# Rotary partners: copies on ScalarE in place of a rotation product on TensorE

## The reference

```python
def apply_rope(x, cos, sin):
    ...
    x1, x2 = x[..., :ROPE_AXIS], x[..., ROPE_AXIS:]      # 32 and 32 of a head's 64
    return jnp.concatenate([x1 * c - x2 * s, x1 * s + x2 * c], axis=-1)

q = apply_rope(rms_norm(q, q_gain), cos, sin) * (HEAD_DIM ** -0.5)
k = apply_rope(rms_norm(k, k_gain), cos, sin)
```

## Time and profile before

| | us |
|---|---|
| median of 3 runs | 1077.39 |
| profiled execution | 1076.99 |
| its span, first to last instruction | 1075.10 |
| TensorE busy | 1055.5 (98%) |
| VectorE busy | 686.2 (64%) |
| ScalarE busy | 547.3 (51%) |
| GpSimd busy | 90.5 (8%) |

### The profile page before, as it was taken

The page is one execution under the profiler, slowest core; times in us unless marked ns, Lnnn a source line. Parts: engine busy times, 40 slices in busy tenths (PEclk is TensorE's granted clock), DMA queues, the critical chain, the costliest instruction groups (busy, mean ns, idle before and its releaser), DMA issues.

```text
span 1075.1 us, 20694 instructions
## 1 busy us (share of the span) xinstructions
PE 1055.5 (98%) x8454; PEld 1025.9 (95%) x8454; DVE 686.2 (64%) x998; ACT 547.3 (51%) x790; POOL 90.5 (8%) x88
## 2 busy tenths in 40 slices
PE   9999999999999999999999999999999999999997
PEld 8999999999779999999999999999999999999986
DVE  6666656467674866664467666644698668667652
ACT  5444444454765544434346444444568846454541
POOL 2100000028000200000011000000224210000000
PEclk9999999999999999999999999999999999999999
DMA  9564446625013255445663564366328525655541
GB/s 299 164 223 159 137 145 204 220 96 171 21 41 127 96 191 176 156 127 188 195 196 118 179 195 155 108 213 208 118 80 268 163 79 181 201 168 195 192 141 39
DMA packets 160910, 170.15 MB, mean 158 GB/s; under 512 B 3264, under 2 KB 154104, under 8 KB 160840
## 3 DMA queue, kind: packets, MB, share of 16 engines
q1 hardware_dynamic: 160456, 168.70, 48.4%
q0 software_dynamic: 96, 0.28, 0.1%
q10 hardware_dynamic: 288, 0.18, 0.1%
HBM read 167.82 MB, written 1.05 MB: 157 GB/s over the span
## 4 chain that ended last, share of the span: by engine, by line
PE 89%; DVE 5%; ACT 3%; DMA 1%; POOL 1%; issue 1%; SPq 0%; DVEq 0%; POOLq 0%; ACTq 0%
PE bank L457 23%; PE bank L459 23%; PE bank L458 23%; PE bank L863 5%; PE bank L665 2%; PE bank L664 2%; PE bank L666 2%; PE bank L476 1%; PE bank L473 1%; PE bank L474 1%; PE weighed L768 1%; DMA raw<-in_rec_w_in 1%; DVE h L1414 1%; PE flipped L756 1%; POOL hacc L1865 1%; DVE xl L1378 1%
## 5 line engine op out<-in xcount | busy, mean ns | idle before, releaser
L1372 DVE TENSOR_TENSOR wl<-raw,wh 128x2048 fp32r<-128x2048 f32 (+2 forms) x164 | 342.2, 2108 | 152.5 <-ACT wh L962 152.2
L457 PE MATMUL bank<-xh,wl 128*128 128x272 f32 (+1 forms) x1488 | 430.6, 289 | 3.4 <-DVE tmp L1442 1.1
L459 PE MATMUL bank<-xh,wh 128*128 128x272 f32 (+1 forms) x1488 | 427.4, 287 | 0.0
L458 PE MATMUL bank<-xl,wh 128*128 128x272 f32 (+1 forms) x1488 | 425.8, 286 | 0.0
L962 ACT ACTIVATE wh<-raw 128x2048 fp32r<-128x2048 f32 (+2 forms) x164 | 282.2, 1745 | 105.3 <-PE bank L459 82.9
L457 PEld LDWEIGHTS bank<-xh,wl 128*128 128x128 f32 x1488 | 280.3, 188 | 5.2 <-issue 2.7
L458 PEld LDWEIGHTS bank<-xl,wh 128*128 128x128 f32 x1488 | 280.3, 188 | 0.0
L459 PEld LDWEIGHTS bank<-xh,wh 128*128 128x128 f32 x1488 | 280.3, 188 | 0.0
L457 PE MATMUL bank<-ah,wl 128*128 128x272 f32 x528 | 152.1, 288 | 0.0
L458 PE MATMUL bank<-al,wh 128*128 128x272 f32 x528 | 151.9, 288 | 0.0
L459 PE MATMUL bank<-ah,wh 128*128 128x272 f32 x528 | 151.7, 287 | 0.0
(11 more groups left out here) (197 smaller groups left out, 1209.9 us busy)
## 6 DMA issues: line engine op xcount, KB each, us to landing
raw<-in_ffn_w_in SPq DMA_DIRECT2D x88, 1024.0 KB, 5.3
raw<-in_ffn_w_out SPq DMA_DIRECT2D x24, 768.0 KB, 4.9
raw<-in_ffn_w_out SPq DMA_DIRECT2D x24, 640.0 KB, 4.4
raw<-in_ffn_w_out SPq DMA_DIRECT2D x10, 1024.0 KB, 5.2
raw<-in_rec_w_in SPq DMA_DIRECT2D x8, 1024.0 KB, 5.5
raw<-in_attn_w_qkv SPq DMA_DIRECT2D x6, 1024.0 KB, 5.0
raw<-in_attn_w_o SPq DMA_DIRECT2D x4, 1024.0 KB, 5.3
raw<-in_rec_gate_w SPq DMA_DIRECT2D x16, 256.0 KB, 5.2
```

The source lines that it names most:

```text
L457: pe.matmul(dst, b, mh, start=first, stop=False)
L458: pe.matmul(dst, a, ml, start=False, stop=False)
L459: return pe.matmul(dst, a, mh, start=False, stop=last)
L1372: dve.tensor_tensor(wl[:, slot(u), 0:kn * 256], w, wh[:, slot(u), 0:kn * 256].bitcast(F32), ALU.subtract).then_inc(w_ready, units)
```

## The change

The rotation product goes. In its place ScalarE copies the partner rows of `qp` into `pad`, in four blocks of 32 partitions and 272 columns for each tile: rows 32 to 63 into 0 to 31, 0 to 31 into 32 to 63, and the same in the upper half. The minus sign moves into the sine table. VectorE's `times_sin` then multiplies `pad` in place, reading it from SBUF instead of the product from PSUM. The wait for `pad` to be free moves from VectorE to ScalarE. The constants lose the rotation matrix. TensorE's program loses the product and its waits.

```diff
-            c[m + half, C_ROT + m] = -1.0
...
-        c[b * half:(b + 1) * half, C_SIN:C_SIN + L] = sin
+        c[b * half:(b + 1) * half, C_SIN:C_SIN + L] = sin if b % 2 else -sin
...
-                def rotate(t):
-                    pe.wait_ge(q_gained, t + 1)
-                    if t:
-                        pe.wait_ge(q_sin, t)
-                    pe.matmul(ROTB[:, 0:L // 2], rotm, qp[:, t % 2, 0:L // 2], start=True, stop=True)
-                    pe.matmul(ROTB[:, L // 2:L], rotm, qp[:, t % 2, L // 2:L], start=True, stop=True).then_inc(q_rot, 1)
...
-                                mean_and_rotation(0)
+                                head_means(0)
...
+                def partners(t):
+
+                    act.wait_ge(q_gained, t + 1)
+                    if t >= 2:
+                        act.wait_ge(q_roped, t - 1)
+                    for a in range(0, P, HD):
+                        for b, c in ((a, a + HD // 2), (a + HD // 2, a)):
+                            last = act.activation(pad[b:b + HD // 2, t % 2, 0:L], qp[c:c + HD // 2, t % 2, :], ACT.Copy)
+                    last.then_inc(q_rot, 1)
...
                 root_of_h(1)
+                partners(0)
                 high(U_QKV + 4, 0, KC, (qk_done, 4))
...
                 root(0)
+                partners(1)
                 squared(2)
                 root(1)
+                partners(2)
                 squared(3)
                 high(U_QKV + 5, 0, KC, (qk_done, 4))
                 root(2)
+                partners(3)
                 squared(4)
                 root(3)
+                partners(4)
                 squared(5)
+                partners(5)
                 high(U_WO, 0, KC, (qk_done, 6))
                 root(4)
                 squared(6)
                 root(5)
+                partners(6)
                 root(6)
                 squared(7)
+                partners(7)
                 high(U_WO + 1, 0, KC, (qk_done, 8))
                 root(7)
                 squared(8)
+                partners(8)
                 root(8)
                 squared(9)
+                partners(9)
                 root(9)
...
                     dve.wait_ge(q_rot, t + 1)
-                    if t >= 2:
-                        dve.wait_ge(q_roped, t - 1)
-                    dve.tensor_tensor(pad[:, t % 2, 0:L], ROTB[:, 0:L], sin, ALU.mult).then_inc(q_sin, 1)
+                    dve.tensor_tensor(pad[:, t % 2, 0:L], pad[:, t % 2, 0:L], sin, ALU.mult).then_inc(q_sin, 1)
```

More of the change, by code:

```diff
@@ L66 @@
 VB = 90
-C_ID, C_ONES, C_BONES, C_ROT, C_COS, C_SIN = 0, P, P + 1, P + 3, 2 * P + 3, 2 * P + 3 + L
-C_N = 2 * P + 3 + 2 * L
+C_ID, C_ONES, C_BONES, C_COS, C_SIN = 0, P, P + 1, P + 3, P + 3 + L
+C_N = P + 3 + 2 * L
 NPROJ = 6
@@ L132, in shape_constants @@
     half = HD // 2
-    for m in range(P):
-        if m % HD < half:
-            c[m + half, C_ROT + m] = -1.0
-        else:
-            c[m - half, C_ROT + m] = 1.0
     for half_tile in range(2):
@@ L224, in build @@
         SC = 384
-        QSUM, ROTB, QSCALE = bank[5], bank[3], bank[6]
+        QSUM, QSCALE = bank[5], bank[6]
         U_VAL = U_QKV + 5
@@ L236, in build @@
         ident = cst[:, C_ID:C_ID + P]
-        rotm = cst[:, C_ROT:C_ROT + P]
         head_mean_w = cst[:, C_BONES:C_BONES + 2]
@@ L388, in vectors @@
                                  gain.rearrange("(a b p) -> a b p", a=1, b=1).broadcast_to([1, 2, HD])).then_inc(s_vec, 16)
-                sp.dma_start(cst[:, C_ROT:C_N], consts[:, C_ROT:C_N]).then_inc(s_rope, 16)
+                sp.dma_start(cst[:, C_COS:C_N], consts[:, C_COS:C_N]).then_inc(s_rope, 16)
             sp.dma_start(tok_in[0:L - 2 * P, 2, :], x[2 * P - META:SEQ, :]).then_inc(s_xin, 16)
@@ L771, in weigh @@
                         last.then_inc(pv_done, 1)
[L773 to L776, removed]
                 def values(c, k):
@@ L800, in attention @@
                             if k == 7:
-                                mean_and_rotation(1)
+                                head_means(1)
                         if t == 5:
@@ L805, in attention @@
                             if k == 3:
-                                mean_and_rotation(2)
+                                head_means(2)
                             if k == 6:
@@ L809, in attention @@
                             if k == 7:
-                                mean_and_rotation(3)
+                                head_means(3)
                         if t == 6:
                             if k == 2:
-                                mean_and_rotation(4)
+                                head_means(4)
                             if k == 6:
-                                mean_and_rotation(5)
+                                head_means(5)
                         if t > 6 and k == 3:
-                            mean_and_rotation(t - 1)
+                            head_means(t - 1)
                         if t == QKT - 1 and k == 6:
@@ L825, in attention @@
                         if (c, k) == (0, 4):
-                            mean_and_rotation(QKT - 1)
+                            head_means(QKT - 1)
                         if (c, k) == (0, 7):
@@ L835, in attention @@
                         pe.wait_ge(q_step, 3 * QKT - 2)
-                        pe.wait_ge(q_sin, QKT)
                         pe.wait_ge(v_ready, 2)
@@ L1313, in recurrent_out @@
                 high(U_FFN[3] + 2, 0)
-            act.dma_start(cst[:, 0:C_ROT], consts[:, 0:C_ROT]).then_inc(s_in, 16)
+            act.dma_start(cst[:, 0:C_COS], consts[:, 0:C_COS]).then_inc(s_in, 16)
             act.dma_start(tok_in[0:META, 0, :], meta).then_inc(s_xin, 16)
@@ L1585, in final @@
                     dve.tensor_tensor(kd[:, 2 * t + 1, :], qn[:, t, :], QSCALE[:, 0:L], ALU.mult).then_inc(q_final, 1)
+                dve.wait_ge(s_rope, 16)
                 rc_of_h(1)
```

## The result

| | before | after |
|---|---|---|
| median of 16 runs | 1077.39 us | 1082.26 us |
| lowest and highest | 1076.43, 1080.35 | 1079.61, 1085.95 |
| profiled execution, its span | 1076.99, 1075.10 | 1082.74, 1080.9 |

The changed kernel takes 1.0044 times as long (95% interval 1.0037 to 1.0051): by the medians 4.9 us more, where 2.2 us less had been predicted. The range ended at 1078.4.

The account below looks back on a forecast made before the run. The prediction took TensorE, busy for 98% of the span, as the bound. Savings of 0.20 before tile 6 and 2.82 after, less 0.8 for a second wait, made -2.2 us: 1075.2 against 1077.39, range 1074.0 to 1078.4.

Parts of the forecast that it names:

- What is removed: TensorE's stream in the attention stage: ten rotations of 0.47 us go, 4.7 us saved.
- the prediction's case in which tile 6 doesn't wait: Rival: a 32-row copy on ScalarE takes only 0.17 us, net -4.3 us, 1073.1; chance 0.05.
- What is added: ScalarE gets 40 copies of 32x272, taken at 0.33 us each because neighbours overlap by 0.09.
- c: Time from one ScalarE partner-row copy to the next, taken as 0.33 us, own range 0.31 to 0.36.
- The rival (c 0.43 to 0.45): ScalarE's copies don't overlap because each starts at other partitions: net +0.2 to +0.7 us, 1077.6 to 1078.1; chance 0.25.
- The wait at tile 6: TensorE waits there for ScalarE's gained copy until 248.75, so the first 1.88 us of savings become 0.20.
- The second wait: TensorE at head_means(8) waits for squared(8), 0 to 0.9 us, taken as 0.8.
- The sum: Savings of 3.0 us less a later wait of 0.8: -2.2 us, 1075.2; chance 0.55.
- no overlap: Rival: ScalarE's copies take 0.43 to 0.45 us each, net +0.2 to +0.7 us; chance 0.25.
- Slower: Rival: ScalarE drains and restarts for each block, 0.53 us per copy, net +2.6 us, 1080.0; chance 0.10.
- Cheap blocks: Rival: a 32-row block costs ScalarE 0.17 us, so tile 6 doesn't wait, net -4.3 us, 1073.1; chance 0.05.
- Swallowed: Rival: the gain is lost after the attention stage in a later wait that isn't TensorE's, 1077.4; chance 0.05.

Follow-up runs that it names:

- e2: Changed kernel without rotation or copies: VectorE multiplies the tile itself by the sine, leaving the partner rows out; 1072.17 us, ratio 0.9963 to the kernel before.
- e3: Kernel before plus 24 ScalarE copies of 272 columns ahead of its first stage, in six groups differing in partition count and start partitions; one execution, 1081.82 us.
- e6: Changed kernel with the same 40 copies all reading and writing partitions 0 to 31, partner rows left out; 1075.99 us, ratio 0.9992 to the kernel before.
- e1: Changed kernel with 15 small fp32 products on TensorE ahead of its wait at tile 6; 1078.53 us, ratio 1.0010 to the kernel before.
- e10: Kernel before with six plain 96x1088 activations on ScalarE ahead of tile 4's square, making tile 6 late; 1083.50 us, ratio 1.0063.
- e5: Changed kernel with the partner rows moved by four DMAs per tile on SyncE's queue instead of ScalarE copies; 1078.91 us, ratio 1.0018 to the kernel before.
- e9: Changed kernel with tiles 0 to 3, 5 and 7 rotated on TensorE, only 4, 6, 8 and 9 copied; 1077.70 us, ratio 1.0001 to the kernel before.
- e7: Changed kernel with tiles 0 to 3 rotated on TensorE again and copies only for tiles 4 to 9; 1075.86 us, ratio 0.9988 to the kernel before.
- e4: Changed kernel with ScalarE's square and gained copy of tile 4 ahead of tile 3's copies and the weight copy; 1078.77 us, ratio 1.0014 to the kernel before.

## Why the prediction was wrong

- **What is removed, 4.7 us.** Right: e2's stage is 4.26 shorter, and the prediction's case in which tile 6 doesn't wait had -4.3.
- **What is added, c = 0.33, "since two neighbours that need not wait for each other overlap by 0.09". This step failed.** The copies take 0.445. All neighbours from which 0.33 was read start at the same partition; the copies never do, and e3 shows that this alone is what takes the overlap away. The rival (c 0.43 to 0.45) named the mechanism and got a quarter of the chance. Its price, 1078.1 at most, was too low, since it too left out the clock and the later waits.
- **The wait at tile 6.** The place was right and the chain too (e6: 13.57, worked out 13.76). With c = 0.445 sixteen copies make it 16 x 0.115 = 1.84 us later, and the squares and roots that stand beside the blocks lose their overlap as well, some 0.8 more (0.42 instead of 0.27, and 0.21 instead of 0.11). In e6, where all starts are the same, they have it again. Why the gained copy waits for the square ahead of it, which starts at the same partition, no run shows. Set to before's start of the stage, tile 6 begins at 252.35 - 0.97 = 251.38 instead of 248.75: 2.63 us.
- **The clock was left out, and no rival had it. This step failed too.** The earlier trace rows show 1.00 everywhere, and I took that as given, though the forecast itself put a wait of 1.7 us where TensorE had not waited. In the profiled execution the fall costs 4.34 us (33.76 against e1's 29.42), between the medians 3.7. It is the largest single term, and the one that put the time well outside the range: with the clock held up, e1 has 1078.53, at the range's end. Even with c as forecast it isn't free: in e6 the clock falls after a wait of 1.43, and by the medians half of the forecast 2.2 us are left.
- **The second wait, 0.8 us.** Too small. At full clock tile 6 to the turn takes 29.42; six rotations less would be 30.19 - 2.82 = 27.37, so 2.05 us of waits are in it. e1's profile lists two there, 0.88 at head_means(6) for VectorE's hq and 0.50 at head_means(8) for ScalarE's square; head_means(8) was the place predicted. The other 0.67 are gaps too short to be listed and slower starts behind waits.
- **The sum**, in the stage: -2.2 forecast, +2.63 for tile 6, +4.34 for the clock, +1.25 for the later waits, together +6.0, as measured in the profiled execution. Without the clock it would still be slower: e1 is 1.6 us over the kernel before, where the rival "no overlap" had +0.2 to +0.7.
- **Rivals.** "Slower" expected +2.6 from a c of 0.53; c is not that, and the loss has another cause. "Cheap blocks" is out: 32 partitions cost the same 0.32 as 128. "Swallowed" is out as well, the stage shows the whole loss.
- **Left open:** why the fallen clock lasts longer in one execution than in another, and which waits bring it on. The changed kernel's runs spread over 6.3 us, and their time goes with their mean clock over the span: 0.992 or 0.993 in the eight up to 1081.96, 0.986 to 0.989 in the three from 1084.90. In the profiled executions the slow stretch lasted about 15 us after a wait of 3.71 and about 7 after 3.08 (e10). It came after a wait of 1.43 in e6, 1.74 in e5 and 2.12 in e9's recurrence. But in the recurrence of e1 a wait of 1.79 left the clock at 1.00, as 1.57 did in the kernel before, where every stretch of 5 us from 10 to 1070 us has 0.98 or more.
The Trainium skill ("TensorE: Matmul & The Clock Gate", What's actually happening) also has the clock at half its rate after idle time. The traces of e10 and of the changed kernel agree. A fall after 1.43 us in one kernel and none after 1.79 in another show that the length of the wait alone doesn't settle it.

## What to carry to other kernels

A product taken from a TensorE that is always busy is only saved if what replaces it arrives in time: work out when the next result that TensorE waits for is ready, with every replacing instruction in the chain, and where that makes a wait, price the granted clock behind it too (here 4 us for a wait of 3.7, and 2.4 for one of 3.1). Read the duration of an added instruction from rows whose operands lie the same way; neighbours that move between partitions need a row of their own, or the price without overlap. Where the slack is only in a part of the stage, make the exchange only there (e7), and expect the last microsecond to drown in what varies elsewhere.

## What the runs showed of the hardware that was not expected

- ScalarE's neighbours of 32x272 follow each other in 0.32 us, and in 0.44 where the input or the output starts at another partition than in the one before (e3). One of the two is enough. 32 partitions take as long as 128.
- TensorE's clock stayed at 0.50 for some 15 us with TensorE busy all the while (252.35 to 267.5). Fifteen small fp32 products in 3.62 us, whose result nobody uses, kept it at 1.00 (e1).
- The fall need not lie in the wait: in e4 the wait ended at 254.06 with the clock at 1.00, a product of 272 columns still took 0.12 us to the next start at 254.96, and from 255.28 on 0.23.
- A DMA of 34 KB from SBUF to SBUF took 1.9 us at the median, and a tile needs four that are issued one after the other, about 0.6 us each; VectorE waited for them for up to 3.9 us (e5).
